# Fused transformer kernel, opening of the first mixer: squared tiles added on GpSimd, first weights split in two parts, products of a cleared tile

## What is computed

```python
def rmsnorm(x, g):
    xf = x.astype(jnp.float32)
    y = xf * lax.rsqrt(jnp.mean(xf * xf, axis=-1, keepdims=True) + EPS) * g.astype(jnp.float32)
    return y.astype(x.dtype)
...
def hybrid_mixer(h, w_in, b_if, conv_q, conv_k, g_head, w_pool, pool_scale, w_br_a, w_br_b, w_out):
    z = h @ w_in
    ...
    u_pool, q, k, v, o, i_pre, f_pre, ga, gb = jnp.split(z, idx, axis=-1)
...
x = x + hybrid_mixer(rmsnorm(x, g_mix[l]), w_in[l], ...)
```

## Time and profile before

| what | value |
|---|---|
| time, median of 3 runs | 3387.36 us (3385.61 to 3387.78) |
| span of the profiled execution | 3381.1 us |
| TensorE busy | 3320.3 us, 98% |
| VectorE busy | 2138.1 us, 63% |
| ScalarE busy | 1604.9 us, 47% |
| GpSimd busy | 166.2 us, 5% |
| moved by DMA | 492.93 MB, mean 146 GB/s |

### The profile page before, as it was taken

One profiled execution on the slowest core, in us unless ns is written; L12 is line 12 of the kernel. 1 busy time (PEld: TensorE's weight loads), 2 busy tenths in 40 slices (PEclk: granted clock), 3 DMA queues, 4 the chain that ended last, 5 costly groups with the idle time before them and its releaser, 6 DMA issues. The chain is left out here.

```text
span 3381.1 us, 55633 instructions
## 1 busy us (share of the span) xinstructions
PE 3320.3 (98%) x23758; PEld 2755.8 (82%) x23758; DVE 2138.1 (63%) x2643; ACT 1604.9 (47%) x1886; POOL 166.2 (5%) x145
## 2 busy tenths in 40 slices
PE   8999999999999998999999999999999999999998
PEld 6987676778888887888888888888788888788887
DVE  6665453469889887756657663555676567763544
ACT  5432111348788875343456553533443455643432
POOL 0000000001011112000000000000000000000000
PEclk9999999999999999999999999999999999999999
DMA  5211442369999997122111111343122111111433
GB/s 224 82 54 57 166 161 79 139 234 405 414 412 418 413 415 286 45 76 88 52 64 51 41 68 50 111 176 131 68 71 77 56 46 58 39 63 51 156 125 112
DMA packets 97243, 492.93 MB, mean 146 GB/s; under 512 B 10920, under 2 KB 11432, under 8 KB 59104
## 3 DMA queue, kind: packets, MB, share of 16 engines
q1 hardware_dynamic: 77216, 417.31, 32.3%
q0 software_dynamic: 14160, 51.55, 4.3%
q10 hardware_dynamic: 5616, 20.45, 1.5%
HBM read 431.43 MB, written 57.84 MB: 145 GB/s over the span
## 5 line engine op out<-in xcount | busy, mean ns | idle before, releaser
L136 PE MATMUL ps<-HH,WS 128*128 128x512 f32 (+1 forms) x2592 | 1032.8, 398 | 4.3 <-DVE WS L1574 2.3
L138 PE MATMUL ps<-HH,WS 128*128 128x512 f32 (+1 forms) x2592 | 1012.2, 390 | 0.0
L137 PE MATMUL ps<-HL,WS 128*128 128x512 f32 (+1 forms) x1952 | 761.7, 390 | 0.0
L136 PEld LDWEIGHTS ps<-HH,WS 128*128 128x128 f32 (+1 forms) x2592 | 486.3, 188 | 111.6 <-DVE WS L1574 5.9
L138 PEld LDWEIGHTS ps<-HH,WS 128*128 128x128 f32 (+1 forms) x2592 | 486.0, 187 | 105.2
L1639 ACT ACTIVATE WA<-ps 128x512 f32<-128x512 f32 x240 | 142.7, 595 | 824.6 <-PE ps L138 797.3
L137 PEld LDWEIGHTS ps<-HL,WS 128*128 128x128 f32 (+1 forms) x1952 | 366.5, 188 | 73.7 <-issue 1.2
L136 PE MATMUL ps<-WAR 128*128 128x512 f32 x768 | 306.9, 400 | 1.3 <-DVE WAR L1368 1.3
L138 PE MATMUL ps<-WAR 128*128 128x512 f32 x768 | 301.3, 392 | 0.0
L1574 DVE TENSOR_TENSOR WS<-RAW,WS 128x1024 fp32r<-128x1024 f32 (+1 forms) x153 | 202.7, 1325 | 118.6 <-ACT WS L1569 118.6
L136 PE MATMUL ps<-WS,HH 128*128 128x256 f32 x896 | 259.3, 289 | 12.6 <-DVE WAR L2564 11.3
(11 more groups left out here) (407 smaller groups left out, 5198.4 us busy)
## 6 DMA issues: line engine op xcount, KB each, us to landing
WR<-in_weu SPq DMA_DIRECT2D x36, 1024.0 KB, 8.8
WR<-in_wed SPq DMA_DIRECT2D x36, 1024.0 KB, 8.5
WR<-in_weg SPq DMA_DIRECT2D x35, 1024.0 KB, 10.0
RAW<-in_wo SPq DMA_DIRECT2D x32, 1024.0 KB, 4.9
WA<-in_wada SPq DMA_DIRECT2D x48, 512.0 KB, 4.5
H<-in_weg SPq DMA_DIRECT2D x23, 1024.0 KB, 9.9
H<-in_weu SPq DMA_DIRECT2D x23, 1024.0 KB, 8.5
H<-in_wed SPq DMA_DIRECT2D x22, 1024.0 KB, 10.0
```

The source lines that it names most:

```text
L136: t.matmul(o, l[0], r[0], start=st, stop=False)
L137: t.matmul(o, l[0], r[1], start=False, stop=False)
L138: return t.matmul(o, l[1], r[0], start=False, stop=sp)
```

## The change

GpSimd clears the tile `zero` as its first operation. TensorE no longer waits for the constants at its beginning; it waits for the cleared tile and multiplies it by itself five times into a bank of its own, without use for the result. The weights of v0 are split in two halves (k 0 to 3, k 4 to 7), each with its own semaphores; VectorE does the second half after the rest of tile 1. GpSimd adds the squared tiles one after another, 7 adds for each half, and TensorE makes one product of ones a half from the last sum: that of i = 0 after k = 0 of the values' second half, that of i = 1 inside the rows' first half after k = 3. `tensor_first_scale(0)` moves to k = 5. The first half of q0 is taken from its place and put between the two halves of the rows. ScalarE and VectorE get a new order: three gained tiles of i = 1 come before root(0), the other five behind it, interleaved with the squares of i = 1 and the roundings of i = 0; root(1) stands before round_(7, 0); the splits of rows and q0 come earlier. VectorE waits for the scale vectors rather than the constants at its beginning. The diff, its unchanged lines cut:

```diff
...
             for j in range(4):
                 wa.take("sq", M, j)
                 wa.take("h", M, j)
+            brief("warm", "start", end=("warm", "start"))
             for i in range(2):
...
             for j in range(4):
-                wa.give(("sq", M, j), ("sq_summed", M, 2 * j + 1, 1))
+                wa.give(("sq", M, j), ("start_added", 2 * j + 2, 1) if j < 3 else ("sq_summed", M, 1))
             for k in range(8):
                 wa.give(("xl", k), ("pj_mm", M, 0, 3))
...
             s.dma_start(MD[:, 64:72], d["cT"]).then_inc(*up("c_in", by=16))
         def mixer_start_tensor(t):
-            for i in range(2):
-                free(t, banks, "rms", M, i)
-        def tensor_start_sum(t, k, i):
-            t.wait_ge(*at("squared", M, k, i))
-            t.matmul(ps("rms", M, i), ones, start_slot("sq", k), start=k == 0, stop=k == 7).then_inc(*up("sq_summed", M, k, i))
+            free(t, banks, "warm", "start")
+            t.wait_ge(*at("zero"))
+            for _ in range(5):
+                o = t.matmul(ps("warm", "start"), tl("zero")[:, 0:128], tl("zero")[:, 0:512], start=True, stop=True)
+            o.then_inc(*up("warm", "start"))
+        def tensor_start_sum(t, i):
+            free(t, banks, "rms", M, i)
+            t.wait_ge(*at("consts", "ct"))
+            t.wait_ge(*at("start_added", 7, i))
+            t.matmul(ps("rms", M, i), ones, start_slot("sq", 7), start=True, stop=True).then_inc(*up("sq_summed", M, i))
+        def tensor_start_rows(t, i):
+            n = tile_no("rows")
+            hi, lo = parts(M, n)
+            t.wait_ge(*at("w_lo", M, n))
+            free(t, banks, "pj", M, n, i)
+            hs = token_half(i)
+            for k in range(8):
+                t.wait_ge(*at("h_lo", M, k, i))
+                o = mm3(t, ps("pj", M, n, i)[0:hi.shape[2], :], (hi[:, k, :], lo[:, k, :]), (HH[:, k, hs], HL[:, k, hs]), k == 0, k == 7)
+                if i == 0 and k == 3:
+                    tensor_start_sum(t, 1)
+            o.then_inc(*up("pj_mm", M, n, i))
+        def gpsimd_start_sums(g, i):
+            for k in range(1, 8):
+                if k == 1:
+                    g.wait_ge(*at("squared", M, 0, i))
+                else:
+                    g.wait_ge(*at("start_added", k - 1, i))
+                g.wait_ge(*at("squared", M, k, i))
+                g.tensor_tensor(start_slot("sq", k), start_slot("sq", k - 1), start_slot("sq", k), ALU.add).then_inc(
+                    *up("start_added", k, i))
         def tensor_first_scale(t, i):
             free(t, banks, "first_scale", i)
...
             def square(k, i):
                 if i:
-                    a.wait_ge(*at("sq_summed", M, k, 0))
+                    a.wait_ge(*(at("start_added", k + 1, 0) if k < 7 else at("sq_summed", M, 0)))
                 a.activation(start_slot("sq", k), X[:, k, i * 512:(i + 1) * 512], ACT.Square).then_inc(*up("squared", M, k, i))
...
                 table_for(a, ACT.Ln)
-                a.wait_ge(*at("sq_summed", M, 7, i))
+                a.wait_ge(*at("sq_summed", M, i))
                 a.activation(r, ps("rms", M, i), ACT.Ln, scale=1.0 / 1024, bias=eps).then_inc(*up("rms_ln", M, i))
                 table_for(a, ACT.Exp)
...
                 a.wait_ge(*at("pj_mm", M, 0, 2 * i + 1))
                 a.activation(HH[:, k, hs], start_slot("h", k), ACT.Copy).then_inc(*up("h_hi", M, k, i))
-            scalar_split(a, M, 0)
+            a.wait_ge(*at(raw_sem(M, 0), M, 0))
+            for part in range(2):
+                free(a, wss, "ws", M, 0, part)
+            for q in range(2):
+                cs = slice(q * 1024, (q + 1) * 1024)
+                a.activation(parts(M, 0)[0][:, cs], raw_of(M, 0)[:, cs], ACT.Copy).then_inc(*up("first_hi", q))
             for k in range(8):
                 gained(k, 0)
                 square(k, 0)
-            for k in range(8):
+            for k in range(3):
                 gained(k, 1)
-            scalar_split(a, M, 1)
-            for k in range(8):
-                square(k, 1)
             root(0)
             for k in range(8):
-                round_(k, 0)
+                if k < 5:
+                    gained(k + 3, 1)
+                square(k, 1)
+                if k == 4:
+                    scalar_split(a, M, 1)
+                if k:
+                    round_(k - 1, 0)
             root(1)
+            round_(7, 0)
+            scalar_split(a, M, 2)
             scalar_first_values(a, 0)
             for k in range(8):
                 round_(k, 1)
-            scalar_split(a, M, 2)
             scalar_first_values(a, 1)
         def scalar_first_values(a, i):
...
                 v.tensor_tensor(HL[:, k, hs], start_slot("h", k), HH[:, k, hs].bitcast(F32), ALU.subtract).then_inc(
                     *up("h_lo", M, k, i))
-            vector_split(v, M, 0)
-            for i in range(2):
-                for k in range(8):
-                    rest_gained(k, i)
-            vector_ones(v, 0)
-            vector_split(v, M, 1)
-            for i in range(2):
-                v.wait_ge(*at("rms", M, i))
-                for k in range(8):
-                    scale(k, i)
-                    if k:
-                        rest(k - 1, i)
-                rest(7, i)
-                if i:
-                    vector_split(v, M, 2)
+            def first_split(q):
+                cs = slice(q * 1024, (q + 1) * 1024)
+                hi, lo = parts(M, 0)
+                v.wait_ge(*at("first_hi", q))
+                v.tensor_tensor(lo[:, cs], raw_of(M, 0)[:, cs], hi[:, cs].bitcast(F32), ALU.subtract).then_inc(
+                    *(up("w_lo", M, 0) if q else up("first_lo", 0)))
+            def first_factor(i):
                 v.wait_ge(*at("first_scale_mm", i))
                 v.tensor_scalar(first_scale[:, 4 * i:4 * i + 4], ps("first_scale", i)[:, 0:4], 1.0, None, ALU.mult).then_inc(
                     *up("first_scale", i))
+            first_split(0)
+            for k in range(8):
+                rest_gained(k, 0)
+                if k == 1:
+                    first_split(1)
+            for k in range(3):
+                rest_gained(k, 1)
+            vector_ones(v, 0)
+            v.wait_ge(*at("consts", "ct"))
+            v.wait_ge(*at("rms", M, 0))
+            for k in range(8):
+                if k < 5:
+                    rest_gained(k + 3, 1)
+                scale(k, 0)
+                if k == 5:
+                    vector_split(v, M, 1)
+                if k:
+                    rest(k - 1, 0)
+            rest(7, 0)
+            vector_split(v, M, 2)
+            first_factor(0)
+            v.wait_ge(*at("rms", M, 1))
+            for k in range(8):
+                scale(k, 1)
+                if k:
+                    rest(k - 1, 1)
+            rest(7, 1)
+            first_factor(1)
         def vector_ones(v, p):
             for j in range(3):
...
         def tensor_mixer_values(t, p):
             n = tile_no(f"v{p}")
             hi, lo = parts(M, n)
-            t.wait_ge(*at("w_lo", M, n))
+            t.wait_ge(*(at("w_lo", M, n) if p else at("first_lo", 0)))
             def product(c, z, k, start, stop):
                 ts = slice((2 * c + z) * 128, (2 * c + z + 1) * 128)
...
                     for c in (2 * i, 2 * i + 1):
                         free(t, banks, "pj", M, n, c)
                     for k in range(8):
+                        if i == 0 and k == 4:
+                            t.wait_ge(*at("w_lo", M, n))
                         t.wait_ge(*at("xg_lo", k, i))
...
                                 o.then_inc(*up("pj_mm", M, n, c))
-                        if i == 0 and k % 4 == 3:
-                            for k_ in range(k - 3, k + 1):
-                                tensor_start_sum(t, k_, 0)
-                        if i and k == 3:
-                            for k_ in range(8):
-                                tensor_start_sum(t, k_, 1)
+                        if i and k == 0:
+                            tensor_start_sum(t, 0)
+                        if i and k == 5:
                             tensor_first_scale(t, 0)
                     yield
...
         def tensor_head(t, h):
             for nm in HEAD:
-                yield from tensor_pass(t, M, tile_no(f"{nm}{h}"))
+                if (h, nm) == (0, "q"):
+                    yield
+                    tensor_half(t, M, tile_no("q0"), 1)
+                    yield
+                else:
+                    yield from tensor_pass(t, M, tile_no(f"{nm}{h}"))
         def scalar_head(a, h):
             for c in range(2):
...
         def mixer_tensor(t):
             mixer_start_tensor(t)
             step_all(tensor_mixer_values(t, 0))
-            tensor_half(t, M, tile_no("rows"), 0, ready=lambda k, i: ("h_lo", M, k, i))
+            tensor_start_rows(t, 0)
             tensor_first_scale(t, 1)
```

(10 more changed lines are left out.)

## The result

Median of the changed kernel: 3391.25 us (3386.95 to 3395.53, 21 runs), beside 3385.94 us (3383.91 to 3390.11, 21 runs) of the kernel before on the same chip. The ratio is 1.0015, 95% interval 1.0009 to 1.0020: 5.3 us longer, within the 0.2% that the prediction called the same. The profiled execution spans 3391.7 us, against 3381.1: 10.6 us, twice the difference of the medians. The two profiles are not of median executions. In all executions whose span is on record the time stands 1.7 to 2.9 us above the execution's own span; so most of the 6.3 us between span and median of the kernel before, which the text ahead takes for work outside the span, is a fast profiled execution.

The account below looks back on a forecast made before the run. TensorE, busy 98% of the span, bounds the kernel; after the change VectorE bounds the opening. k0 1.4 us later plus 1.6 us for the clock gives +3.0 on 3387.4: 3390.4 us, range 3378.5 to 3396.5.

Parts of the forecast that it names:

- TensorE's removal: In the opening, 16 products of ones become 2, taking 12.2 us off TensorE, all on the path.
- the first product: TensorE's first product of the values starts at 10.15 us instead of 11.35, 1.2 us earlier.
- The new bound: Ahead of k0, VectorE takes over from TensorE; with free adds k0 starts at 66.2 us, 8.0 us earlier.
- The text's 66.2: Time in us when k0's products could start if GpSimd's adds cost VectorE nothing; 74.21 before.
- Exclusion: In the opening, GpSimd's adds and VectorE's operations hold each other 1.17 us in turns: k0 +3.7 and +5.7 us.
- Rival (a): In the opening, no exclusion where it counts, adds falling into VectorE's waits: -7.9 us, 3379.5 us; chance 17%.
- Rival (b): In the opening, GpSimd never waits and delays only operations starting under it: k0 at 72.0, 3386.0 us; chance 18%.
- Rival (c): In the opening's second half, half clock around rows adds 3.6 us, longer holds 2.0: 3396.0 us; chance 19%.
- holds of 1.29 us: In the opening, each add holds VectorE for its whole recorded length: 2.0 us more than the forecast sum.
- Clock: Behind TensorE's pause ahead of k0, the granted clock falls to 0.50 and k0's products cost 1.6 us more.

Follow-up runs that it names:

- e1: Changed kernel with GpSimd's 14 adds replaced by 14 fills that read nothing (sums left out): median 3383.06 us, 3.9 us under the kernel before.
- e4: Changed kernel plus 14 unused products filling TensorE's pause ahead of k0: median 3385.33 us, 1.6 us under the kernel before.
- e8: Changed kernel's order with all 16 products of ones left on TensorE and no adds: 2.1 us over the kernel before (ratio 1.0003 to 1.0021).
- e11: Changed kernel with GpSimd copying one tile instead of adding two (sums wrong): 0.1 us under the kernel before (ratio 0.9989 to 1.0007).
- e3: Changed kernel with GpSimd adding the first half only, the second summed by eight products of ones on TensorE: median 3386.43 us, 0.5 us under the kernel before.
- e5: Changed kernel with VectorE's split of k0 moved ahead of the last pair of head sums: 3.9 us over the kernel before (ratio 1.0003 to 1.0021).
- e7: Changed kernel with adds on VectorE, root(1) behind the rounding of tile 7, and k0's split earlier: median 3386.01 us, 0.8 us under the kernel before.
- e12: e10 with og0's split also moved earlier on ScalarE and VectorE: 3386.1 us, 0.1 us under the kernel before.
- e10: e7 plus 18 products of 8 columns behind those of the cleared tile: median 3385.63 us, 0.5 us under the kernel before.
- e6: Changed kernel plus 18 products of 8 columns behind those of the cleared tile: median 3388.54 us, 1.8 us over the kernel before.
- e9: Changed kernel with the five products of the cleared tile 8 columns wide instead of 512: 5.4 us over the kernel before (ratio 1.0008 to 1.0026).

## Why the prediction was right, and where not

**TensorE's removal and the first product.** 2 products of ones instead of 16, first product at 10.30 (10.15 forecast).

**The new bound.** VectorE takes over, as forecast; e1 shows the case without exclusion at 65.5 (66.2 forecast). The text's 66.2 does not follow from its own terms: 55.5, 8.5 us of head sums and rows, and 1.3 us from the split's start to k0 (73.58 to 74.86 in the changed kernel) make 65.3. With that the sum for k0 is 65.3 + 3.7 + 5.7 = 74.7, and 74.9 was measured. The split of k0 starts at 73.58 (74.3 forecast), and TensorE pauses for 3.34 us, not for the 4.5 between 71.1 and 75.6.

**Exclusion.** Forecast: 1.17 us each way, in turns. Measured: 1.05 us on the operations in the loop, 1.12 (2.35 − 1.23) on the split, and GpSimd waits for VectorE. rms(0) at 29.4 (29.1 forecast), the last rest of the first half ends at 52.3 (42.6 + 3.7 + 5.7 = 52.0), k0 at 74.9 (75.6). Rival (a) is what e1 does and the changed kernel doesn't. Rival (b), GpSimd never waits, falls by the 1.71 us between adds, and its k0 at 72.0 wasn't met. Rival (c)'s condition, a granted clock of 0.50 between 45 and 50 us, wasn't met: it was 1.00 there. The 2.0 us that the text adds for holds of 1.29 us are too many: 14 x 0.12 makes 1.7.

**Clock.** The mechanism was there (0.50 in 75 to 80 us behind the pause), the size was mis-sized: 1.6 us forecast, 2.6 by e4. k0 is 0.65 us later than before (+1.4 forecast) and the other 2.85 us of the +3.5 at the scores go to the low clock behind k0; +3.0 was forecast for the two. e8 and e11, with the same pause and a granted clock of 1.00 behind it, show that the term could as well have been 0; that it came is in part luck.

**What was not in the sum.** The text said that after the opening nothing of it is lost or added. Between the scores and 2600 us that held for this pair of executions (+3.5 and +4.1). It does not hold in general: from the scores to 2600 us e3 loses another 8.7 us, e5 4.9 and e7 3.8, e8 and e11 none. The losses stand where the granted clock is under 1 in one execution and 1.00 in another (in 1355 to 1370 us e3 has 0.77 and the kernel before 1.00; in 2425 to 2440, 0.84 and 1.00). One profile of each kernel cannot tell whether that belongs to the kernel or to the execution. The stall in the burst of small products did not come from a time but from the length of TensorE's program, and no row of before could show it. A straight-line fit of the fourteen median differences (the kernel before at 0) to two causes and a constant gives 0.69 ± 0.13 us for each us by which the rows turn later, 2.7 ± 0.8 us for the stall, and 0.5 ± 0.6 for the constant; without a constant the stall gets 3.1 ± 0.6. For the changed kernel: 0.69 x 3.5 + 2.7 = 5.1 of the 5.3 us. So by the fit about half of the measured difference is the mechanism that was forecast, and half is one that was not. This is argued and not shown: the fit takes one profile for each kernel, it leaves 1.5 us unexplained in a typical median, and it prices the stall under the 5.0 us that it costs in the changed kernel's trace. Why a us of the opening is worth less than a us at the end stays open; the losses ahead of 2600 us are a candidate.

That 3391.25 us lies 0.9 from the forecast 3390.4 is partly luck. The kernel before measured 1.4 us less on this chip than the 3387.4 that the forecast starts from, and the difference is 2.3 us larger than the 3.0 forecast.

## What to carry to other kernels

Work that goes from a busy engine to an idle one must be priced on the third engine too: look in the trace for what that idle engine's operations do to those that start beside them, before the move. Taking 12 us off TensorE gave no measurable gain in any version that computes the sums, as the path went over to VectorE at once, and each later repair (e3, e5, e12) uncovered the wait behind it; count how long the other engine's own chain is. Filler products in a pause are cheap if they fit into it (e4: 0.18 us of waiting left) and dear if they run past it (e10: 3.3 us). An edit that changes the number of instructions can move a stall far behind it, so look for one before a small difference is put down to the edit itself.

## What the hardware showed that was not expected

- TensorE stands still for 2.6 to 3.4 us in a dense burst of small products in seven kernels, and goes on 1.3 to 1.5 us after a block of instructions (0.02 MB, on the queue for instructions) has landed; in the seven kernels without the stall a block had come 7.9 to 10.5 us ahead of the burst. It goes with the length of the program: 14 instructions more at the start of the kernel (e4) and it is gone 2.6 ms later. That the missing block is the cause is read from when it comes, at this one place of the program.
- Tiny products keep TensorE busy in the records, yet the granted clock fell behind them in all three kernels that have the 18 of them (0.80 in 10 to 15 us in e6, 0.76 in e10, 0.83 in e12; 1.00 in the changed kernel and in e7).
- The same pause of 3.3 us ahead of k0 was followed by a granted clock of 0.50 (changed kernel), 0.72 (e6), 0.76 (e9) or 1.00 (e8) in 75 to 80 us.
